# Retention heads of a hybrid encoder layer: the rotation's exchanged halves come by DMA instead of by ScalarE's copies

## What is computed

```python
def apply_rotary(t, cos, sin):
    t1, t2 = t[..., :C_DK // 2], t[..., C_DK // 2:]
    c, s = cos[None, :, None, :], sin[None, :, None, :]
    return jnp.concatenate([t1 * c - t2 * s, t1 * s + t2 * c], axis=-1)

def retention_group(q, k, v, cos, sin):
    q = apply_rotary(q.astype(f32).reshape(bsz, s, C_HEADS, C_DK), cos, sin)
    k = apply_rotary(k.astype(f32).reshape(bsz, s, C_HEADS, C_DK), cos, sin) * (C_DK ** -0.5)
    ...
    scores = jnp.einsum('bhnik,bhnjk->bhnij', qc, kc) * decay_mask[None, :, None]
    o_intra = jnp.einsum('bhnij,bhnjv->bhniv', scores, vc)
    ...
    o = o_intra + jnp.einsum('bhnik,bhnkv->bhniv', q_dec, prev_state)
    o = o * lax.rsqrt(jnp.mean(o * o, axis=-1, keepdims=True) + EPS)

h = rmsnorm(x, norm_gain)
proj = jnp.einsum('bsd,de->bse', h, w_in)
y = jnp.concatenate([ya, yb, yc], axis=-1)
return x + jnp.einsum('bse,ed->bsd', y, w_out)
```

## Time and profile before

| what | value |
|---|---|
| median of 3 runs | 1773.1 us (1772.71 to 1775.99) |
| profiled execution, its own time | 1771.2 us |
| its span, first to last instruction | 1769.4 us |
| mean granted TensorE clock | 0.991 of full speed |
| busy share of TensorE, VectorE, GpSimd, ScalarE | 97%, 66%, 47%, 38% |
| mean DMA rate over the span | 235 GB/s |

### The profile page before, as it was taken

The page is one execution under the profiler, slowest core; times in us unless marked ns, Lnnn a source line. Parts: engine busy times, 40 slices in busy tenths (PEclk is TensorE's granted clock), DMA queues, the critical chain, the costliest instruction groups (busy, mean ns, idle before and its releaser), DMA issues. The chain is left out here.

```text
span 1769.4 us, 28242 instructions
## 1 busy us (share of the span) xinstructions
PE 1714.2 (97%) x10536; PEld 1416.7 (80%) x10536; DVE 1165.2 (66%) x1721; ACT 674.5 (38%) x1037; POOL 839.6 (47%) x601
## 2 busy tenths in 40 slices
PE   7999999999999999999999889999999999999996
PEld 6888888888888788888787668888888877888885
DVE  7866565554656555656569876787655448777886
ACT  4423344332422355444553423432334233333442
POOL 4544454544444766656534354444444330355452
PEclk9999999999999999999999999999999999999998
DMA  7999798886998767766777832333333269778876
GB/s 254 328 319 350 253 319 279 297 303 233 331 341 316 255 220 245 259 229 232 247 247 257 306 121 85 104 101 103 97 111 122 77 205 348 249 251 258 281 251 232
DMA packets 216012, 416.47 MB, mean 235 GB/s; under 512 B 24506, under 2 KB 25279, under 8 KB 215876
## 3 DMA queue, kind: packets, MB, share of 16 engines
q1 hardware_dynamic: 201322, 368.56, 61.4%
q10 hardware_dynamic: 14554, 46.10, 7.5%
HBM read 339.05 MB, written 75.51 MB: 234 GB/s over the span
## 5 line engine op out<-in xcount | busy, mean ns | idle before, releaser
L890 POOL TENSOR_TENSOR w_sum<-in_raw,in_raw 128x512 f32<-128x512 f32 x220 | 305.2, 1388 | 298.1 <-PE prj L941 149.0
L941 PE MATMUL prj<-in_hi,w_hi 128*128 128x512 f32 x840 | 329.1, 392 | 10.2 <-DVE w_lo L1943 9.7
L941 PE MATMUL prj<-in_lo,w_hi 128*128 128x512 f32 x840 | 327.8, 390 | 0.0
L941 PE MATMUL prj<-in_hi,w_lo 128*128 128x512 f32 x840 | 327.6, 390 | 0.0
L908 POOL TENSOR_SCALAR w_hi<-w_sum 128x512 fp32r<-128x512 f32 x63 | 101.8, 1616 | 257.9 <-DMA w_sum<-in_w 240.4
L1365 ACT ACTIVATE w_hi<-w_sum 128x512 fp32r<-128x512 f32 x220 | 136.0, 626 | 164.3 <-POOL w_sum L890 163.1
L941 PEld LDWEIGHTS prj<-in_hi,w_hi 128*128 128x128 f32 x840 | 158.2, 188 | 45.3 <-issue 10.1
L901 POOL TENSOR_TENSOR w_lo<-in_raw,w_hi 128x512 fp32r<-128x512 f32 x88 | 119.4, 1362 | 150.0 <-ACT w_hi L1365 150.0
L917 POOL TENSOR_TENSOR raws<-raws 128x512 f32<-128x512 f32 x80 | 111.8, 1399 | 164.0 <-DMA raws<-in_wo 163.9
L941 PEld LDWEIGHTS prj<-in_lo,w_hi 128*128 128x128 f32 x840 | 158.2, 188 | 33.2 <-issue 0.5
L941 PEld LDWEIGHTS prj<-in_hi,w_lo 128*128 128x128 f32 x840 | 158.2, 188 | 32.8
(11 more groups left out here) (183 smaller groups left out, 3021.1 us busy)
## 6 DMA issues: line engine op xcount, KB each, us to landing
in_raw<-in_wi SPq DMA_DIRECT2D x528, 256.0 KB, 4.5
raws<-in_wo SPq DMA_DIRECT2D x184, 256.0 KB, 3.7
arena<-z_scratch ACTq DMA_DIRECT2D x56, 512.0 KB, 4.5
z_scratch<-acc_in SPq DMA_DIRECT2D x88, 256.0 KB, 4.7
y_in<-y_scratch SPq DMA_DIRECT2D x80, 256.0 KB, 4.6
mv_hi<-comb_scratch SPq DMA_DIRECT2D x72, 256.0 KB, 4.5
mv_lo<-comb_scratch SPq DMA_DIRECT2D x72, 256.0 KB, 5.3
w_sum<-in_w SPq DMA_DIRECT2D x60, 256.0 KB, 2.9
```

The source lines that it names most:

```text
L890: nc.gpsimd.tensor_tensor(w_sum[wslot(n)][:], in_raw_buf(a), in_raw_buf(b), ALU.add if sign > 0 else ALU.subtract).then_inc(in_wsum, 1)
L941: last = nc.tensor.matmul(out, wt[wslot(n)][:, i % GRAN, :], mv[j % 2][:, i, :], start=(i == 0 and wt is w_hi and mv is in_hi), stop=(i == ...
```

## The change

For heads 0 to 3 ScalarE's four copies are gone. `load_qk` issues, directly behind the load of CQK, four DMAs of 32 partitions (128 KB each) that read the same tile of the scratch with the halves exchanged, into T3. The sign moves into the table of sines. `rotate` waits for these four (64 counts a head). Since the DMAs bring unscaled data, heads 2 and 3 no longer scale CQK after landing, but multiply the rotated sum by the RMS factor. VectorE still writes a pad column when CQK has landed (`qk_landed`). In `b_unit` of the last attention head the load of CQK now stands behind the wait for the last scores, as T3 is used by that head (BQH). Head 4 keeps its four copies, without the sign.

```diff
-    sin = np.tile(np.sin(ang).astype(np.float32).T, (4, 1))
+    sin = np.sin(ang).astype(np.float32).T
+    sin = np.concatenate([-sin, sin, -sin, sin])
...
+            def load_qk(i):
+                t = c_tile(i)
+                load_z(t, CQK, z0_in)
+                for t1 in (0, C_DK):
+                    t2, end = t1 + C_DK // 2, t1 + C_DK
+                    act.dma_start(arena[t1:t2, T3, :], z_dram[t][t2:end, :]).then_inc(c_partner, 16)
+                    act.dma_start(arena[t2:end, T3, :], z_dram[t][t1:t2, :]).then_inc(c_partner, 16)
...
                     if n == BLK:
-                        load_z(b_tile(i + 1) if not last else c_tile(0), BQ, z0_in)
+                        if not last:
+                            load_z(b_tile(i + 1), BQ, z0_in)
                         act.wait_ge(drained[0], b_m0(i) + 1 + BLK)
                         if last:
+                            load_qk(0)
                             act.dma_start(arr(CSIN), rot_d[1]).then_inc(ctab_in, 16)
                             act.dma_start(arr(CCOS), rot_d[0]).then_inc(ctab_in, 16)
...
-                        load_z(c_tile(i + 1), CQK, z0_in)
-                        until(b + 2)
-                        partner(i + 1)
+                        load_qk(i + 1)
...
-                load_z(c_tile(i), CQK, z0_in)
+                load_qk(i)
...
-                partner(i)
...
-            partner(0)
...
+            def qk_landed(i):
+                dve.wait_ge(z0_in, 16 * (c_pos(i) + 1))
+                nc.vector.memset(land_pad[:, c_tile(i) % 30:c_tile(i) % 30 + 1], 0.0).then_inc(cq_ready, 1)
...
             def rotate(i):
-                dve.wait_ge(c_partner, 4 * i + 4)
+                dve.wait_ge(c_partner, 64 * (i + 1) if i < C_HEADS - 1 else 64 * i + 4)
                 tt(arr(T3), arr(T3), arr(CSIN), ALU.mult).then_inc(c_sin, 1)
                 tt(arr(CQK), arr(CQK), arr(CCOS), ALU.mult).then_inc(c_cos, 1)
                 dve.wait_ge(c_cos, i + 1)
                 dve.wait_ge(c_sin, i + 1)
-                tt(arr(CQK), arr(CQK), arr(T3), ALU.add).then_inc(c_rot, 1)
+                if i < EARLY or i == C_HEADS - 1:
+                    tt(arr(CQK), arr(CQK), arr(T3), ALU.add).then_inc(c_rot, 1)
+                    return
+                tt(arr(CQK), arr(CQK), arr(T3), ALU.add).then_inc(c_sum, 1)
+                dve.wait_ge(c_sum, i - EARLY + 1)
+                tt(arr(CQK), arr(CQK), rstd[:], ALU.mult).then_inc(c_rot, 1)
```

## The result

| what | before | after |
|---|---|---|
| median of the comparison | 1773.09 us (1770.26 to 1779.74, 22 runs) | 1778.27 us (1773.17 to 1783.11, 22 runs) |
| ratio, 95% interval | | 1.0026, 1.0018 to 1.0034 |
| span of the profiled execution | 1769.4 us | 1773.2 us |
| mean granted TensorE clock | 0.991 | 0.991 |

The kernel became slower by 0.26%, 4.6 us by the ratio, with an interval of 3.2 to 6.0 us. The forecast was 1773.1 us with a range up to 1776.8; the result lies outside.

What follows compares the result with a forecast made beforehand. The prediction took TensorE, 97% busy, as the bound, with head 0's 3.34 us stall hanging on VectorE's rotation end, not on the copies. All terms were 0, summing to 0 us: forecast 1773.1 us, range 1770.3 to 1776.8.

Steps and rivals of the forecast that it cites:

- The second price: Behind head 0's stall: lowered TensorE clock makes 12 matmuls take 5.26 us against 2.85 for the next 12, 2.4 us more.
- The copies that nobody waits for: Heads 0 to 3: 16 of ScalarE's 20 copies go, 17.0 us busy time, none on TensorE's path; term 0.
- Head 0, the rotation's start: Four pieces cost 2.0 us, cosines land at 851.9, 0.5 us before wanted; term 0, upper bound landing 1.5 us late.
- the port rule: Head 0: loads to partitions 0 to 31 get about half rate, so pieces take 4.0 us, 1.5 us late; set aside.
- The issues: Head 0: four more DMA issues at 0.5 us make 2.0 us, overlapping earlier transfers, so not added.
- Head 1: Pieces taken as in time for the rotation at 880.32; even late ones not waited for by TensorE; term 0.
- Head 2: Multiply moved ahead of second `part_low`, which ends at 1326.9, 0.5 us before TensorE reads it; term 0, bound +0.8 us.
- Head 3: Rotation starts 2.0 us earlier, has one step of 1.2 us more, ends 0.8 us earlier; term 0.
- Head 4: Keeps its copies, so VectorE's 4.18 us and TensorE's 1.79 us waits stay; term 0.
- Rival 3: Head 0: pieces cost double, by issue or ports, 1.5 us, giving 1774.6 us; chance 0.20.
- the collision: Head 2: the new multiply waits for GpSimd, `part_low` ends at 1328.3, +0.8 us, 1775.4 us with the doubled pieces.
- Rival 4: Head 0: pieces don't overlap, cosines land at 858.3, VectorE stands 5.9 us, giving 1779.0 us; chance 0.08.

Runs made afterwards that it cites:

- e8: Kernel before with the sign in the sine table, no DMA for the halves, VectorE making two of head 4's four copies: ratio 0.9989 (0.9976 to 1.0002).
- e7: Against the kernel before, DMA at head 0 alone, as one 128-partition load without exchanging halves, in place of four pieces: ratio 1.0002 (0.9992 to 1.0012).
- e12: Against the kernel before, DMA at heads 1 and 3 only, head 4's copies shared with VectorE: ratio 1.0000 (0.9991 to 1.0010).
- e10: Against the kernel before, exchanged halves by DMA at head 1 alone, copies at the other heads: ratio 1.0000 (0.9987 to 1.0013).
- e13: Changed kernel with copies kept at head 0 and head 2's multiplication behind the second `part_low`; against the kernel before: ratio 1.0007 (0.9996 to 1.0017).
- e11: e8 run once more, against the kernel before: ratio 0.9996 (0.9987 to 1.0005).
- e5: Against the kernel before, exchanged halves by DMA (four pieces) at head 0 alone, copies at the other heads: ratio 1.0018 (1.0005 to 1.0030).
- e9: Against the kernel before, DMA at head 0 alone, as two 64-partition loads without the exchange, in place of four pieces: ratio 1.0006 (0.9992 to 1.0020).
- e14: The changed kernel run once more, unaltered, against the kernel before: ratio 1.0022 (1.0012 to 1.0032).

## Why the prediction was wrong, point by point

- **What bounds the kernel** was right: the stall at head 0 hangs on the rotation's end, and each us by which the rotation is late is a us of TensorE. Idle times of 0.65, 1.36, 1.37, 2.03 and 2.56 us in front of it went with waits of 4.1, 4.8, 4.8, 5.5 and 6.0 us, that is 0.7, 1.5, 1.5, 2.1 and 2.6 above 3.34. The second price, 2.4 us of lower clock behind the stall, was one execution's value; it ran from nothing (e8) to those 2.4 us.
- **The copies that nobody waits for**: right. Sixteen of them went, and no version without them at some head is shown to be faster. ScalarE's 18.5 us were worth nothing.
- **Head 0, the rotation's start** is the step that failed; with head 2 below it makes the greater part of the loss. It said: "2.0 us for a further 512 KB in that burst", and took 2.0 us for the four pieces. The 2.0 us are the price of 512 KB in one load of 128 partitions: e7 has a lag of 1.7 us against a mean of -0.3 in the nine profiles with copies at head 0, about 2.0 us. With the four pieces the lag is 2.6 to 4.6 us in five profiles, 3.6 on the mean, so that they cost 3.9 us. The upper bound, "+4.0 us, landing at 853.9, which is 1.5 us late", was the value to take. I took the row nearest in place and time, and passed over that it differs in shape. The prediction's own sentence on the port rule gave 4.0 us and 1.5 us late; measured are 3.9 us and, on the mean, 1.7. That "no row of this trace has a transfer of 32 full rows to test it" was a reason to leave the question open, not to give the rule a chance of 0.20.
- **The issues** were costed at 0.5 us each and hidden; they took 0.44 to 0.49 us at head 0, the first one 0.99. Hidden behind transfers or not, they are contained in the lag. Long issues aren't the pieces' own: e8, without any, has one of 1.23 us for the first table.
- **Head 1** was right: the load came later in this profile (the changed kernel's issue at 869.50 landed after 6.5 us, before 4.4; with the pieces behind it, it took 4.1 us in e12 and 7.5 in e10), the rotation began at 880.31 without idle, and TensorE waited for none of it; e10 has the ratio 1.0000.
- **Head 2** failed, and the way in which it failed is worth more than its size. The bound was "+0.8 us" with the argument that "`part_low` at 1325.64, with both inputs in SBUF, ran inside that stretch in 0.69 us, so by this row nothing is blocked". The row was right and is repeated by e13, but it speaks of GpSimd's rounding, a TENSOR_SCALAR. The instruction behind it, a TENSOR_TENSOR, does exclude VectorE's, and the changed kernel moved `part_low` by enough to meet that one.
  The size comes out in two parts. With the rule, the prediction let `part_low` end at 1328.3, 3.3 us behind VectorE's release at 1325.03; measured is 1331.03, 3.25 us behind the end of the rotation at 1327.78. That part has the size of the bound's +0.8, by luck: the bound let the multiplication wait for the rounding, while in fact the multiplication ran beside the rounding in 1.51 us and `part_low` was held by the subtraction. But TensorE came earlier by this clock: 2.47 us behind the rotation's end before (1327.50 less 1325.03), 1.89 now (1331.08 less 1.41 less 1327.78), because the first `part_low` had delayed the rotation by 0.73 us. Together 1.4 us. That first collision stems from the traffic that the prediction costed at head 0 and 1 only.
  The Trainium skill (SBUF — State Buffer, "Who interferes with whom") gave the rule that I set aside, that a VectorE instruction with two inputs in SBUF and a GpSimd one that reads SBUF exclude each other. For the subtraction the trace agrees with it, in both directions, and the kernel before had the row, `part_low` in 1.44 us at head 3. For the rounding, with its one input, the trace differs: VectorE's instructions took 0.69 to 0.83 us beside it (0.69 alone) and 1.51 (1.21 alone), and the rounding was stretched. The measurement decides.
- **Head 3** had the right term, 0, but not the right course. The rotation, counted from the issue of the head's load, started 1.4 us earlier and not 2.0, and ended 0.9 us later and not 0.8 earlier: GpSimd's next subtraction held the multiplication, which took 2.20 us. TensorE has no wait for it, since `part_low` was still 2.8 us ahead of its reader. VectorE's timeline of the changed kernel:

```profile
1355.44 2.20 DVE L2377 TENSOR_TENSOR arena<-arena,rstd 128x1024 f32<-128x1024 f32 x1
```

- **Head 4** was right. Its wait of 1.8 us stayed, and that it can be had by splitting the copies (e8, e11) moved the time by less than can be measured.
- **The chances.** Rival 3 with the collision gave 1775.4 us against the 1778.27. It had both mechanisms, with the right places, and had 0.20. Rival 4, at 0.08, comes nearer with 1779.0 us, but by luck: it wanted the cosines at 858.3 and VectorE idle for 5.9 us, measured are 851.9 and 0.65 us, 2.56 us at the most in five profiles. Its size was 2.3 us in place of the 3.0 that the waits sum to and the 4.6 measured. Slower by over 0.2% had 0.08. The range ended at 1776.8, with the head-0 term at its one value of 1.5 us; it was between 0.7 and 2.6 us in five profiles.

## What to carry to other kernels

Before a cheap-looking DMA is costed by its bytes, look at how many partitions one load covers: where the queues are full, a cut into pieces of 32 or 64 partitions cost 1.6 to 2 times what the same bytes cost in one load (3.3 and 3.9 us against 2.0), for itself and for what is issued behind it. When a row says that two engines don't disturb each other, it says so for those two kinds of instruction; look which instruction comes next on the other engine, since a step that is moved by a us meets that one, and look for the same pair elsewhere in the trace: the row was there, at head 3. And work that is hidden on an idle engine is worth nothing to remove: here the copies were free, and their replacement used the one resource, the DMA queue at head 0, that had 2.5 us left.

## What the runs showed of the hardware that was not expected

- The DMA engines show a busy share of 1.0 both at 387 to 411 GB/s and, with pieces under way, at 251 to 309 GB/s (844 to 848) or 225 (846 to 848, e5); the busy share doesn't tell whether the queues deliver. The rate beside it does.
- A piece of 64 partitions gains little over one of 32: 226 GB/s against 225 in the windows on them (e9, e5), a lag of 3.0 us against 2.6 to 4.6.
- The exclusion between VectorE and GpSimd goes both ways, and whoever is first keeps its time: `part_low` 1.78 us behind a subtraction (0.69 alone), the subtraction 1.86 us behind a multiplication (1.27 alone). Beside a TENSOR_SCALAR of GpSimd `part_low` took 0.69 to 0.83, and the TENSOR_SCALAR itself 2.05 to 2.36 (1.49 alone), 4.61 at head 3 of the changed kernel and 5.08 in e14.
- The first of the four issues at head 0 took 0.99 us in the changed kernel and 0.51 to 1.42 in the others with four pieces, the further ones mostly 0.44 to 0.5.
